# An encoder layer with 32 experts: the experts' tokens gathered in f32 instead of three bf16 parts, and a third place for weights outside the ring

## The chip, the cores and the metric

The kernel runs on one core of a Trainium2 chip. The metric is the device time of one execution in microseconds (us), the median of three timed runs. One further execution was profiled.

## The reference

One encoder layer over 256 tokens of width 1024, all in float32:

```
n = rms_norm(h);  z = n @ w_in                      # 1024 -> 2336 columns
o = concat(bidirectional gated linear attention, grouped-query attention)
h = h + o @ w_out
x = rms_norm(h);  logits = x @ w_router + b_router  # 32 experts
top 4 of 32 experts per token, softmax over the 4
for each expert e, over the tokens that chose it:
    a = x @ w1[e] + b1[e]                           # 1024 -> 2048: glu | lin
    glu = min(a[:, :1024], 7);  lin = clip(a[:, 1024:], -7, 7)
    y = (glu * sigmoid(1.702 * glu) * (lin + 1)) @ w2[e] + b2[e]
h = h + sum over a token's experts of gate * y
out = rms_norm(h)
```

The weights of the experts are 32 x 12.58 MB = 402.7 MB, all of which are read from HBM once.

## The kernel before

**Stages.** The projections and both attentions run first, from 0 to about 120 us. The output projection adds into `h` (2 tiles of 128 tokens, kept in f32 in SBUF), the router picks the experts, and then the 32 experts run one after the other. Each takes up to 64 of its tokens (`CAP`); further rounds would follow if an expert had more, and there are none here.

**Chunks and places.** The weights of an expert come in six chunks of 2 MB (four of `w1`, two of `w2`; chunk c belongs to expert c // 6). `ring` has eight places (`SLOTS`). A place is free again when TensorE has used its chunk and raised `chunk_used`; SyncE waits for that and issues the next load. Its loads are processed in order. Chunks 0 to 7 are loaded before the experts start, each as soon as the part of `ring` that `w_in` or `w_out` held is free. Two more places lie in `work`: `EARLY = 2` chunks, 19 and 20 (`EARLY_AT`), go there, also before the experts start. They are used once. So chunks 8 to 18 wait for the chunk 8 before them, chunks 21 to 28 for the one 10 before them (`SLOTS + EARLY`), and from chunk 29 on (`PEELED`) each waits for the chunk 8 before it again. The first two bodies of four experts (48 chunks) are written out; from chunk 48 a loop loads pairs of 4 MB; the last body is written out again, its last three chunks in halves. In the last body, experts 28 and 29 also add rows to the output (`add_row` L1511, `add_h` L1550), four times each.

**The gather.** TensorE gathers an expert's tokens with a one-hot matrix: weights are 128 tokens x 128 columns of the normed `h`, the moving operand is `onehot` (128 tokens x 64 places), the result 128 x 64 in a PSUM bank, for 8 column groups (`KD`) and 2 token tiles. Column groups take every fourth column, to match how `w1`'s rows lie in the chunks. To keep f32 precision with bf16 matmuls, the normed `h` is held as the sum of three bf16 parts (`PARTS`): `part0` in `work`, the other two in `tok`. So a gather is 8 x 3 x 2 = 48 matmuls (L1543). The parts are made ahead of expert 0: token tile 0 by ACT (L595), DVE (L993) and POOL (L453, L455), tile 1 in halves by ACT (L605, L610) and DVE (L1005, L1011). The first gather is in quarters (`first_gather(half, t)`, L1529): three before expert 0 starts, the fourth after its first chunk. DVE multiplies the result with the norm's gain into `xg` (L1065; L1073 for the first).

**One expert on TensorE.** Bias (L1471), 64 passes of the first layer (L1641), the gather of the next expert, the combine of the last one's result (L1555), the turns of the hidden values (L1667, once DVE's L1095 is done) and of the gates (L1676), 32 passes of the second layer (L1685). Meanwhile DVE clips (L1089, L1090), multiplies (L1092, L1095) and makes the masks (L1082, L1058), and ACT takes the sigmoid (L620) into `sig`. Before the first gather TensorE runs four matmuls whose result isn't used (`keep_busy`, L1477). The router's sum is one matmul per token tile (L1437).

Of the kernel before, what the change touches and what calls it, by code (L numbers as in the profile page):

```python
# [22 lines left out]
BF16 = mybir.dt.bfloat16  # L23
# [45 lines left out]
EARLY = 2  # L69
EARLY_AT = 19  # L70
FINE = (3, 4, 5)
# [12 lines left out]
assert W2_RUN * P == FF and (WRITTEN * PER_BODY - EARLY) % PAIR == 0  # L84
# [34 lines left out]
def encoder_layer(nc, x, w_in, w_out, w_router, w1, b1, w2, b2, gate_w, columns, rows, final_g,  # L119
                  c_keep, c_front, later, split, out):  # L120
    ctx = ExitStack()
    with ctx:
# [19 lines left out]
        wr_sb = sb("wr_sb", [P, KD, EXPERTS])  # L142
        col = sb("col", [P, 2 * KD + 4])
# [6 lines left out]
        class Carve:  # L150
# [70 lines left out]

        early = [work[:, KD * SEQ + i * SLOT:KD * SEQ + (i + 1) * SLOT] for i in range(EARLY)]

# [6 lines left out]
        onehot = back(TILES * CAP // 2).bitcast(BF16).rearrange("p (t c) -> p t c", c=CAP)  # L230
        gated = back(TILES, P)
        gatedT = back(TILES, P)
        xg = back(KD * CAP)
        assert back.at <= KD * SEQ

        back = Carve(work, KD * SEQ + EARLY * SLOT)
# [3 lines left out]
        sig = back(FG)  # L240
        hidT = back(SUB, P)
        part0 = back(TILES * D // 2).bitcast(BF16).rearrange("p (t d) -> p t d", d=D)
        part_sb = back(TILES, P)
        gateT = part_sb.rearrange("p t c -> p (t c)")
        res = back(D // GROUPS)
        reuse = Carve(work, at_glu)
        left = reuse(TILES, D)
# [3 lines left out]
        parts12 = tok.bitcast(BF16).rearrange("p t (i d) -> p t i d", i=PARTS - 1)  # L251
        parts = [[part0[:, t, :]] + [parts12[:, t, i, :] for i in range(PARTS - 1)] for t in range(TILES)]
        hT = [turned[:, :, 0:P], tok[:, 1, :].rearrange("p (k t) -> p k t", t=P)]
# [12 lines left out]
            part0_t0 left_t0 part1_t0 part2_t0 part0_t1 left_t1 part1_t1 part2_t1  # L266
# [19 lines left out]
        def slot_of(c):  # L286

            return (c - EARLY) % SLOTS

        def first_slot_of(c):  # L290

            return c % SLOTS
# [9 lines left out]
        def by_row(chunk, width):  # L302

            return chunk.rearrange("p (r n) -> p r n", n=width)
# [3 lines left out]
        def _(sp):  # L308
# [46 lines left out]
            def first_ring(s):  # L355
                load(slot(s), slot_in[s], s // PER_EXPERT, s % PER_EXPERT)
# [13 lines left out]
            for i in range(EARLY):  # L370
# [48 lines left out]
        def _(pool):  # L419
# [28 lines left out]
            for t in range(TILES):  # L448
                pool.wait_ge(S.var2, t + 1)
                rsqrt(stat[:, 4 + t:5 + t], stat[:, 2 + t:3 + t], 1).then_inc(S.rstd2, 1)  # L450
                if t == 0:
                    pool.wait_ge(S.left_t0, 1)
                    pool.tensor_copy(parts[0][1], left[:, 0, :]).then_inc(S.part1_t0, 1)  # L453
                    pool.wait_ge(S.part1_t0, 1)
                    pool.tensor_tensor(parts[0][2], left[:, 0, :], parts[0][1], ALU.subtract).then_inc(S.part2_t0, 1)  # L455
# [6 lines left out]
        def _(act):  # L462
# [113 lines left out]
            def square(t, nb):  # L576
                act.wait_ge(S.h_done, 2 * t + nb + 1)
                cols = slice(nb * 512, (nb + 1) * 512)
                nc.scalar.activation(left[:, t, cols], h[:, t, cols], ACT.Square,
                                     accum_out=stat[:, 8 + 2 * t + nb:9 + 2 * t + nb]).then_inc(S.hsq, 1)  # L580
# [13 lines left out]
            act.wait_ge(S.rstd2, 1)  # L594
            nc.scalar.activation(parts[0][0], h[:, 0, :], ACT.Copy, scale=stat[:, 4:5]).then_inc(S.part0_t0, 1)  # L595
# [5 lines left out]

            act.wait_ge(S.rstd2, 2)
            for nb in range(2):
                cols = slice(nb * 512, (nb + 1) * 512)
                nc.scalar.activation(parts[1][0][:, cols], h[:, 1, cols], ACT.Copy, scale=stat[:, 5:6]).then_inc(S.part0_t1, 1)  # L605
            act.wait_ge(S.parts_ps, 2)
            for nb in range(2):
                cols = slice(nb * 512, (nb + 1) * 512)
                act.wait_ge(S.left_t1, nb + 1)
                nc.scalar.activation(parts[1][1][:, cols], left[:, 1, cols], ACT.Copy).then_inc(S.part1_t1, 1)  # L610
# [34 lines left out]
            for i in range(GROUPS):  # L645
                act.wait_ge(S.glu_ready, final + (i + 1))
                nc.scalar.activation(halves(sig, i), halves(glu, i), ACT.Sigmoid, scale=ALPHA).then_inc(S.sig_ready, 1)
# [24 lines left out]
        def _(dve):  # L672
# [300 lines left out]
            def choose(t):  # L973
# [18 lines left out]
            dve.wait_ge(S.part0_t0, 1)  # L992
            nc.vector.scalar_tensor_tensor(left[:, 0, :], h[:, 0, :], stat[:, 4:5], parts[0][0], ALU.mult, ALU.subtract)\  # L993
                .then_inc(S.left_t0, 1)
# [7 lines left out]
            def left_over(nb):  # L1002
                cols = slice(nb * 512, (nb + 1) * 512)
                dve.wait_ge(S.part0_t1, nb + 1)
                nc.vector.scalar_tensor_tensor(left[:, 1, cols], h[:, 1, cols], stat[:, 5:6], parts[1][0][:, cols],  # L1005
                                               ALU.mult, ALU.subtract).then_inc(S.left_t1, 1)

            def last_part(nb):
                cols = slice(nb * 512, (nb + 1) * 512)
                dve.wait_ge(S.part1_t1, nb + 1)  # L1010
                nc.vector.tensor_tensor(parts[1][2][:, cols], left[:, 1, cols], parts[1][1][:, cols], ALU.subtract)\  # L1011
                    .then_inc(S.part2_t1, 1)

            left_over(0)

            def first_mask(t):
# [3 lines left out]
                nc.vector.tensor_scalar(onehot[:, t, :], slots[:, 0:CAP], rank_t[:, t, 0:1], None, ALU.is_equal)\  # L1020
# [57 lines left out]
            def expert(n):  # L1078
# [16 lines left out]
                nc.vector.tensor_tensor(lin, lin, sig, ALU.mult).then_inc(S.hid_ready, 1)  # L1095
# [5 lines left out]
            last_part(0)  # L1101
            half_out(0, 3)
            left_over(1)
            last_part(1)
# [24 lines left out]
            for i in range(GROUPS):  # L1129
# [7 lines left out]
                nc.vector.tensor_tensor(lin_i, lin_i, halves(sig, i), ALU.mult).then_inc(S.hid_ready, 1)  # L1137
# [35 lines left out]
        def _(pe):  # L1173
# [340 lines left out]
            def rows_of(t, i, k):  # L1514

                c, r = divmod(k, W1_ROWS)
                return parts[t][i].rearrange("p (c m r) -> p c m r", m=P, r=W1_RUN)[:, c // PAIR, :, c % PAIR * W1_ROWS + r]

            def first_gather(half, t):
# [3 lines left out]
                for i in range(PARTS):  # L1523
                    if t == 1:
                        pe.wait_ge((S.part0_t1, S.part1_t1, S.part2_t1)[i], half + 1)
                    elif half == 0:
                        pe.wait_ge((S.part0_t0, S.part1_t0, S.part2_t0)[i], 1)
                    for k in range(half * KD // 2, (half + 1) * KD // 2):
# [225 lines left out]
```

## Time and profile before

| | before |
|---|---|
| median of three timed runs | 1059.65 us (1057.33 to 1059.96) |
| profiled execution | 1057.77 us |
| its span, first to last instruction | 1056.0 us |
| mean granted TensorE clock | 0.985 of full speed |
| TensorE busy with passes / with weight loads | 988.4 us (94%) / 439.8 us (42%) |
| DVE, ACT, POOL busy | 223.9, 119.0, 16.6 us |
| moved by DMA | 421.50 MB, 399 GB/s over the span |

Busy time is the union of an engine's instructions; it says that an engine had something in flight, not that it was at its peak. In the trace PE stands for TensorE's passes and PEld for its weight loads, which overlap the passes.
### The profile page before, as it was taken

The page shows a single profiled execution, that of the slowest core. Times are in us where ns is not written, and L with a number is a line of the kernel's source. Part 1 is how long each engine was busy: PE and PEld are TensorE (multiplying, and loading weights), DVE is VectorE, ACT ScalarE, POOL GpSimd, SP SyncE. Part 2 cuts the span into 40 slices and gives each one's busy share as a digit, 9 for nine tenths or more (in the row PEclk, how much of TensorE's full clock was granted, in tenths as well). Part 3 has the DMA queues.
Part 4 walks back from the last instruction along what each step waited for, and adds up shares of the span by engine and source line. Part 5 has one row for each costly group of instructions (what it writes and reads, how often), then busy time and mean ns, then how long its engine had stood idle before and what let it go on. Part 6 is the DMA issues. An engine that isn't in the chain of part 4 may idle for free.

```text
span 1056.0 us, 13569 instructions
## 1 busy us (share of the span) xinstructions
PE 988.4 (94%) x5863; PEld 439.8 (42%) x5863; DVE 223.9 (21%) x525; ACT 119.0 (11%) x235; POOL 16.6 (2%) x19
## 2 busy tenths in 40 slices
PE   7999999999999998899898999889999898999996
PEld 5745544444444443334333433334333343433442
DVE  1786341111111111111111111011111111101112
ACT  1055130000000000000000000000000000000002
POOL 0010110000000000000000000000000000000000
PEclk9999999999999999999999999999999999999999
DMA  9917869999999999999999999999999999999994
GB/s 357 270 42 319 367 239 431 426 426 422 428 426 434 433 429 429 433 429 434 429 434 429 434 429 433 431 433 429 433 432 432 431 432 433 425 430 426 427 423 185
DMA packets 25233, 421.50 MB, mean 399 GB/s; under 512 B 4176, under 2 KB 4688, under 8 KB 6800
## 3 DMA queue, kind: packets, MB, share of 16 engines
q1 hardware_dynamic: 25200, 421.01, 94.6%
q8 instruction: 26, 0.43, 0.2%
q14 instruction: 7, 0.06, 0.0%
HBM read 419.95 MB, written 1.05 MB: 399 GB/s over the span
## 4 chain that ended last, share of the span: by engine, by line
PE 65%; DMA 29%; ACT 2%; DVE 2%; issue 1%; POOL 1%; SPq 0%; POOLq 0%; DVEq 0%
PE bank L1641 30%; DMA ring<-in_w_dram 29%; PE bank L1685 14%; PE bank L1555 4%; PE bank L1205 3%; PE bank L1543 3%; PE bank L1667 1%; PE bank L1446 1%; PE bank L1277 1%; ACT work L623 1%; PE bank L1374 1%; PE bank L1471 1%; PE bank L1601 1%; PE bank L1246 1%; DMA col<-in_columns_dram 1%
## 5 line engine op out<-in xcount | busy, mean ns | idle before, releaser
L1641 PE MATMUL bank<-ring,work 128*64 128x512 f32 x2016 | 460.7, 609 | 33.2 <-DMA ring<-in_w_dram 33.0
L1641 PEld LDWEIGHTS bank<-ring,work 128*64 128x64 f32 x2016 | 176.7, 139 | 297.1 <-issue 242.2
L1685 PE MATMUL bank<-ring,work 128*64 128x512 f32 x992 | 219.7, 595 | 14.9 <-ACT work L623 14.9
L1089 DVE TENSOR_SCALAR work<-bank 128x512 f32<-128x512 f32 x31 | 21.4, 692 | 687.6 <-PE bank L1641 687.6
L1685 PEld LDWEIGHTS bank<-ring,work 128*64 128x64 f32 x992 | 68.9, 137 | 145.8 <-issue 127.5
L620 ACT ACTIVATE work<-work 128x512 f32<-128x512 f32 x31 | 19.7, 634 | 501.8 <-DVE work L1089 501.8
L1555 PE MATMUL bank<-work 64*128 64x512 f32 x256 | 63.6, 615 | 0.7 <-ACT work L655 0.7
L1543 PE MATMUL bank<-work,tok 128*128 128x64 bf16 x992 | 51.3, 197 | 0.0
L1543 PE MATMUL bank<-work 128*128 128x64 bf16 x496 | 50.0, 197 | 0.0
L1543 PEld LDWEIGHTS bank<-work,tok 128*128 128x128 bf16 x992 | 48.8, 116 | 0.0
L1543 PEld LDWEIGHTS bank<-work 128*128 128x128 bf16 x496 | 36.5, 116 | 24.8 <-issue 24.8
L631 ACT ACTIVATE work<-bank 128x512 f32<-128x512 f32 x31 | 18.5, 597 | 214.6 <-PE bank L1685 214.6
L1555 PEld LDWEIGHTS bank<-work 64*128 64x128 f32 x256 | 22.0, 186 | 18.7 <-issue 15.9
L623 ACT ACTIVATE work<-bank 128x512 f32<-128x512 f32 x31 | 18.5, 597 | 91.6 <-PE bank L1667 91.6
L1667 PEld LDWEIGHTS bank<-ckeep,work 128*128 128x128 f32 x124 | 17.3, 210 | 24.0 <-DVE work L1095 22.5
L1082 DVE TENSOR_SCALAR work<-ckeep,work 128x128 f32<-128x128 f32 x62 | 18.7, 344 | 34.8 <-PE bank L1676 34.8
L427 POOL TENSOR_TENSOR stat<-stat 128x1 f32<-128x1 f32 (+2 forms) x8 | 9.7, 1211 | 959.3 <-DVE stat L682 943.0
L1667 PE MATMUL bank<-ckeep,work 128*128 128x128 f32 x124 | 23.2, 310 | 1.2 <-DVE work L1095 1.2
L1092 DVE SCALAR_TENSOR_TENSOR work<-work 128x512 f32<-128x512 f32 x31 | 21.5, 693 | 1.1
L1095 DVE TENSOR_TENSOR work<-work 128x512 f32<-128x512 f32 x31 | 21.5, 692 | 1.1
L1065 DVE TENSOR_TENSOR work<-bank,ffn_pairs 128x512 f32<-128x512 f32 x31 | 21.2, 684 | 0.0
L1090 DVE TENSOR_SCALAR work<-bank 128x512 f32<-128x512 f32 x31 | 21.1, 681 | 0.0
(221 smaller groups left out, 505.2 us busy)
## 6 DMA issues: line engine op xcount, KB each, us to landing
ring<-in_w_dram SPq DMA_DIRECT2D x60, 4096.0 KB, 29.8
ring<-in_w_dram SPq DMA_DIRECT2D x67, 2048.0 KB, 16.4
ring<-in_w_in_dram SPq DMA_DIRECT2D x8, 1168.0 KB, 15.9
ring<-in_w_dram SPq DMA_DIRECT2D x6, 1024.0 KB, 29.8
work<-in_w_dram SPq DMA_DIRECT2D x2, 2048.0 KB, 14.7
ring<-in_w_out_dram SPq DMA_DIRECT2D x2, 1024.0 KB, 10.7
ring<-in_w_out_dram SPq DMA_DIRECT2D x1, 2048.0 KB, 16.8
h<-in_x_dram SPq DMA_DIRECT2D x2, 512.0 KB, 4.2
```

What stands on the lines that cost most here:

```text
L623: nc.scalar.activation(hidT, bank[5][:, :].rearrange("p (s q) -> p s q", q=P), ACT.Copy)\
L1065: nc.vector.tensor_tensor(xg.rearrange("p (k c) -> p k c", c=CAP), bank[6][:, :].rearrange("p (k c) -> p k c", c=CAP), ffn_pairs.rearrange ...
L1089: nc.vector.tensor_scalar(glu, bank[2][:, :], LIMIT, None, ALU.min).then_inc(S.glu_ready, 1)
L1090: nc.vector.tensor_scalar(lin, bank[5][:, :], LIMIT, -LIMIT, ALU.min, ALU.max).then_inc(S.dve_step, 1)
L1092: nc.vector.scalar_tensor_tensor(lin, lin, 1.0, glu, ALU.add, ALU.mult).then_inc(S.dve_step, 1)
L1095: nc.vector.tensor_tensor(lin, lin, sig, ALU.mult).then_inc(S.hid_ready, 1)
L1205: return mm(o, l, r, start=a and first, stop=z, skip_group_check=True)
L1543: last = mm(bank[6][:, k * CAP:(k + 1) * CAP], rows_of(t, i, k), onehot[:, t, :], start=i == 0 and t == 0, stop=i == PARTS - 1 and t == TI ...
L1555: last = mm(bank[Y[i]][:, :], gatedT[j * CAP:(j + 1) * CAP, t, :], res[j * CAP:(j + 1) * CAP, :], start=start, stop=stop, skip_group_check ...
L1641: last = mm(bank[(2, 5)[g]][j * CAP:(j + 1) * CAP, :], xg[:, k * CAP:(k + 1) * CAP], of_group(chunk[:, r, :], g, j), start=False, stop=k = ...
L1667: last = nc.tensor.transpose(bank[5][:, r * P:(r + 1) * P], apart[:, :, r], ident)
L1685: last = mm(bank[6][j * CAP:(j + 1) * CAP, :], hidT[:, r, s * CAP:(s + 1) * CAP], chunk[:, r, j * 512:(j + 1) * 512], start=s == 0 and r == 0,
```

## The change

The experts' gather reads f32 tokens from `h` itself. The factor 1/rms of a token, which was in the parts, moves into the one-hot columns: they become f32, with 1/rms (`stat[:, 4 + t]`) where there was 1. A gather is 8 x 2 = 16 f32 matmuls, and the three parts are not made. The room of the parts in `tok` and `work` becomes a third place outside the ring (`EARLY = 3`, chunk 21): half of it in `tok`, half in `work`, loaded by two DMAs of 1 MB (`load_split`). SyncE issues them after TensorE has turned the first attention's result (`glaT_ps`), between the loads of ring places 6 and 7. To make room, the sigmoid (`sig`) goes to PSUM bank 2, and the squares of h to PSUM banks 2 and 5. The ring is turned by one place (`TURN`): chunk 7 goes to place 0, chunk c to place c + 1.

```diff
-EARLY = 2
+EARLY = 3
+TURN = 1
...
-        onehot = back(TILES * CAP // 2).bitcast(BF16).rearrange("p (t c) -> p t c", c=CAP)
+        onehot = back(TILES, CAP)
...
             def slot_of(c):
-            return (c - EARLY) % SLOTS
+            return (c - EARLY + TURN) % SLOTS
...
+            def load_split(i):
+                e, r = divmod(EARLY_AT + i, PER_EXPERT)
+                assert r < W1_CHUNKS
+                n = SLOT // W1_ROWS
+                for j in range(W1_ROWS):
+                    at = r % PAIR * SLOT + j * n
+                    sp.dma_start(early_rows[j], rows_of(e, r)[:, at:at + n]).then_inc(early_in[i], 16)
...
             sp.wait_ge(S.att_used, 1)
             first_ring(6)
+            sp.wait_ge(S.glaT_ps, TILES)
+            load_split(EARLY - 1)
             sp.wait_ge(S.h_ps, 2 * TILES)
             first_ring(7)
...
-                nc.scalar.activation(left[:, t, cols], h[:, t, cols], ACT.Square,
+                nc.scalar.activation(bank[MIX[nb]][:, :], h[:, t, cols], ACT.Square,
...
-            act.wait_ge(S.rstd2, 1)
-            nc.scalar.activation(parts[0][0], h[:, 0, :], ACT.Copy, scale=stat[:, 4:5]).then_inc(S.part0_t0, 1)
...
-                nc.scalar.activation(sig, glu, ACT.Sigmoid, scale=ALPHA).then_inc(S.sig_ready, 1)
+                nc.scalar.activation(bank[2][:, :], glu, ACT.Sigmoid, scale=ALPHA).then_inc(S.sig_ready, 1)
...
-                    last = nc.vector.tensor_scalar(onehot[:, t, :], slots[:, 0:CAP], rank_t[:, t, bass.ds(n, 1)], None,
-                                                   ALU.is_equal)
+                    last = nc.vector.tensor_scalar(onehot[:, t, :], slots[:, 0:CAP], rank_t[:, t, bass.ds(n, 1)],
+                                                   stat[:, 4 + t:5 + t], ALU.is_equal, ALU.mult)
...
             first_mask(0)
             first_mask(1)
-            last_part(0)
             half_out(0, 3)
-            left_over(1)
-            last_part(1)
             tables()
...
                 for k in range(KD):
-                    for i in range(PARTS):
-                        for t in range(TILES):
-                            last = mm(bank[6][:, k * CAP:(k + 1) * CAP], rows_of(t, i, k), onehot[:, t, :],
-                                      start=i == 0 and t == 0, stop=i == PARTS - 1 and t == TILES - 1)
+                    for t in range(TILES):
+                        last = mm(bank[6][:, k * CAP:(k + 1) * CAP], tokens_of(t, k), onehot[:, t, :],
+                                  start=t == 0, stop=t == TILES - 1)
```

## Rows read from the trace of the kernel before

**Rows 1.** The page: TensorE's busy time, and GB/s in 40 slices of 26.4 us.
```profile
PE 988.4 (94%) x5863; PEld 439.8 (42%) x5863; DVE 223.9 (21%) x525; ACT 119.0 (11%) x235; POOL 16.6 (2%) x19
...
GB/s 357 270 42 319 367 239 431 426 426 422 428 426 434 433 429 429 433 429 434 429 434 429 434 429 433 431 433 429 433 432 432 431 432 433 425 430 426 427 423 185
```

**Rows 2.** The chain that ended last, in order: start us, us, what.
```profile
170.06 13.79 PE bank L1641 x64
183.84 1.67 PE bank L1543 x48
...
196.34 13.79 PE bank L1641 x64
...
445.59 8.83 PE bank L1641 x32
...
912.47 7.14 PE bank L1641 x32
...
935.59 1.05 PE bank L1511 x2
...
1007.97 1.67 PE bank L1543 x48
...
1020.47 13.79 PE bank L1641 x64
```

**Rows 3.** Who waited for whom: total us, times, longest.
```profile
PE bank L1641 <- DMA ring<-in_w_dram: 33.0, 18, 2.6
```

**Rows 4.** Stretches: length, busy by engine, granted clock, DMA share, GB/s.
```profile
108.00:150.00 42.00, 40.31 (x220) 20.61 (x220) 18.98 (x58) 12.82 (x24) 7.36 (x6) 1.00 0.68 276
...
134.00:143.00 9.00, 7.75 (x106) 5.45 (x104) 6.54 (x25) 3.73 (x8) 3.73 (x3) 1.00 0.61 234
...
445.60:454.40 8.80, 8.80 (x33) 3.07 (x34) 0.00 (x0) 0.00 (x0) 0.00 (x0) 0.81 0.99 428
```

**Rows 5.** Runs of f32 weight loads, timeline of several windows: start us, us, what.
```profile
93.40 0.52 PEld L1360 LDWEIGHTS bank<-ring 64*128 64x128 f32 x8
...
104.78 3.54 PEld L1367 LDWEIGHTS bank<-work 128*128 128x128 f32 x31 [0.24 <-issue]
...
136.58 0.30 PEld L1437 LDWEIGHTS bank<-ckeep,work 128*128 128x128 f32 x2
...
140.05 0.97 PEld L1477 LDWEIGHTS bank<-h,ckeep 128*128 128x128 f32 x8
...
544.28 0.56 PEld L1667 LDWEIGHTS bank<-ckeep,work 128*128 128x128 f32 x4 [0.76 <-DVE work L1095]
```

**Rows 6.** Timeline around the start of the experts.
```profile
140.53 0.19 DVE L1018 SCALAR_TENSOR_TENSOR work<-bank,work 128x32 f32<-128x32 f32 x1
...
142.12 0.32 PE L1529 MATMUL bank<-work,tok 128*128 128x64 bf16 x4 [0.21 <-DVE tok L1011]
...
142.96 3.70 PE L1641 MATMUL bank<-ring,work 128*64 128x512 f32 x16
...
161.08 0.75 PE L1667 MATMUL bank<-ckeep,work 128*128 128x128 f32 x4 [1.16 <-DVE work L1095]
```

**Rows 7.** Loads by SyncE: issues, and landing of those at 135.44 and 245.07.
```profile
118.84 16.93 SPq L346 DMA_DIRECT2D ring<-in_w_dram  x2
...
DMA to landing us min/median/max: 7.3/7.3/7.3
...
245.07 0.33 SPq L346 DMA_DIRECT2D ring<-in_w_dram  x1
...
DMA to landing us min/median/max: 8.9/8.9/8.9
```

**Rows 8.** The page's costliest groups: three of DVE and ACT.
```profile
L1089 DVE TENSOR_SCALAR work<-bank 128x512 f32<-128x512 f32 x31 | 21.4, 692 | 687.6 <-PE bank L1641 687.6
...
L620 ACT ACTIVATE work<-work 128x512 f32<-128x512 f32 x31 | 19.7, 634 | 501.8 <-DVE work L1089 501.8
...
L1082 DVE TENSOR_SCALAR work<-ckeep,work 128x128 f32<-128x128 f32 x62 | 18.7, 344 | 34.8 <-PE bank L1676 34.8
```

More of the change, by code:

```diff
@@ L218, in encoder_layer @@
         w_out_gla = ring[:, 7 * SLOT:8 * SLOT].rearrange("p (k n) -> p k n", n=D)
-        early = [work[:, KD * SEQ + i * SLOT:KD * SEQ + (i + 1) * SLOT] for i in range(EARLY)]
+        early = [work[:, KD * SEQ + i * SLOT:KD * SEQ + (i + 1) * SLOT] for i in range(EARLY - 1)]
+        at_split = KD * SEQ + (EARLY - 1) * SLOT
+        early_rows = [tok.rearrange("p t d -> p (t d)"), work[:, at_split:at_split + SLOT // W1_ROWS]]
         back = Carve(work)
@@ L239, in encoder_layer @@
         lin = back(FG)
-        sig = back(FG)
-        hidT = back(SUB, P)
-        part0 = back(TILES * D // 2).bitcast(BF16).rearrange("p (t d) -> p t d", d=D)
         part_sb = back(TILES, P)
         gateT = part_sb.rearrange("p t c -> p (t c)")
-        res = back(D // GROUPS)
-        reuse = Carve(work, at_glu)
-        left = reuse(TILES, D)
+        hidT = back(SUB, P)
+        left = Carve(work, at_split)(TILES, D)
         assert back.at <= WORK
         b1_wide = tok.rearrange("p t d -> p (t d)")
-        parts12 = tok.bitcast(BF16).rearrange("p t (i d) -> p t i d", i=PARTS - 1)
-        parts = [[part0[:, t, :]] + [parts12[:, t, i, :] for i in range(PARTS - 1)] for t in range(TILES)]
-        hT = [turned[:, :, 0:P], tok[:, 1, :].rearrange("p (k t) -> p k t", t=P)]
+        hT = [turned[:, :, 0:P], Carve(work, at_glu)(KD, P)]
         ffn_pairs = sb("ffn_pairs", [P, KD])
@@ L300, in halves, with row_of @@
             return tile.rearrange("p (m r) -> p m r", r=W2_ROWS)[:, :, i * n:(i + 1) * n]
-        def by_row(chunk, width):
-            return chunk.rearrange("p (r n) -> p r n", n=width)
+        def row_of(chunk, r, width):
+            return chunk[r] if isinstance(chunk, list) else chunk[:, r * width:(r + 1) * width]
         @block.sync
@@ L369, in _ @@
             sp.wait_ge(S.ogla_ps, 1)
-            for i in range(EARLY):
+            for i in range(EARLY - 1):
                 load_early(i)
@@ L600, in _ @@
             router_parts(1)
[L602 to L610, printed above, removed]
             for t in range(TILES):
@@ L646, in _ @@
                 act.wait_ge(S.glu_ready, final + (i + 1))
-                nc.scalar.activation(halves(sig, i), halves(glu, i), ACT.Sigmoid, scale=ALPHA).then_inc(S.sig_ready, 1)
+                nc.scalar.activation(halves(bank[2][:, :], i), halves(glu, i), ACT.Sigmoid, scale=ALPHA).then_inc(S.sig_ready, 1)
                 act.wait_ge(S.hidT_ps, final + (i + 1))
@@ L1000, in _ @@
             choose(1)
[L1002 to L1014, printed above, removed]
             def first_mask(t):
@@ L1522, in first_gather @@
                 pe.wait_ge((S.onehot_first, S.onehot_ready)[t], 1)
-                for i in range(PARTS):
[L1524 to L1528, printed above, removed]
-                        last = mm(bank[(3, 6)[half]][:, k * CAP:(k + 1) * CAP], rows_of(t, i, k), onehot[:, t, :],
-                                  start=t == 0 and i == 0 and k % 4 == 0, stop=t == TILES - 1 and i == PARTS - 1,
-                                  skip_group_check=True)
+                for k in range(half * KD // 2, (half + 1) * KD // 2):
+                    last = mm(bank[(3, 6)[half]][:, k * CAP:(k + 1) * CAP], tokens_of(t, k), onehot[:, t, :],
+                              start=t == 0 and k % 4 == 0, stop=t == TILES - 1, skip_group_check=True)
                 if t == 1:
@@ L1598, in second_layer @@
                 def second_layer(s, r):
-                    chunk = by_row(slot_for(q, W1_CHUNKS + s), D)
+                    chunk = slot_for(q, W1_CHUNKS + s)
                     for j in range(GROUPS):
                         last = mm(bank[6][j * CAP:(j + 1) * CAP, :], hidT[:, r, s * CAP:(s + 1) * CAP],
-                                  chunk[:, r, j * 512:(j + 1) * 512], start=s == 0 and r == 0,
+                                  row_of(chunk, r, D)[:, j * 512:(j + 1) * 512], start=s == 0 and r == 0,
                                   stop=s == W2_CHUNKS - 1 and r == W2_ROWS - 1, skip_group_check=True)
@@ L1641, in expert @@
                                 last = mm(bank[(2, 5)[g]][j * CAP:(j + 1) * CAP, :], xg[:, k * CAP:(k + 1) * CAP],
-                                          of_group(chunk[:, r, :], g, j), start=False, stop=k == KD - 1,
+                                          of_group(row_of(chunk, r, 2 * FF), g, j), start=False, stop=k == KD - 1,
                                           skip_group_check=True)
@@ L1681, in expert @@
                 for s in range(W2_CHUNKS):
-                    chunk = by_row(loaded(q, W1_CHUNKS + s, it, final_body), D)
+                    chunk = loaded(q, W1_CHUNKS + s, it, final_body)
                     for r in range(W2_ROWS):
@@ L1685, in expert @@
                             last = mm(bank[6][j * CAP:(j + 1) * CAP, :], hidT[:, r, s * CAP:(s + 1) * CAP],
-                                      chunk[:, r, j * 512:(j + 1) * 512], start=s == 0 and r == 0,
+                                      row_of(chunk, r, D)[:, j * 512:(j + 1) * 512], start=s == 0 and r == 0,
                                       stop=s == W2_CHUNKS - 1 and r == W2_ROWS - 1, skip_group_check=True)
```

46 lines of the change are left out of this document (21 added, 25 removed).

## The prediction

> **What bounds the kernel now.** The engine summary and the 40 slices come first [rows 1]: the reader is to see TensorE busy for 94% and the transfers near 430 GB/s in nearly every slice from the seventh on. Two resources are close to full, so a share of busy time decides nothing, and the chain in order of time comes next [rows 2]. In the early experts it holds compute alone. One expert there takes 196.34 - 170.06 = 26.28 us: 13.79 for the first layer, 1.67 for the gather (the piece at 183.84), and the rest. Later, pieces "DMA ring" come in ahead of first-layer pieces like that of 445.59, and TensorE finds a chunk missing once in two experts. The waits list books 33.0 us of it [rows 3]. The rest is the clock: in 445.60 to 454.40, after such a wait, 0.81 was granted [rows 4], and 32 passes took 8.83 us instead of 7.14 [rows 2]. Together they are what is left when compute is taken out: expert 31's first layer starts at 1020.47, 850.4 us after expert 1's. Thirty experts at 26.28 are 788.4, and the extra rows of the last body add eight times 1.05 [rows 2] = 8.4; 850.4 - 796.8 = 53.6 us were lost to waits and slow clock. The transfers set that pace: 912.47 - 445.59 = 466.9 us for 16 experts, 29.18 each. So TensorE has 2.9 us to spare per expert in the middle. It has none in the first experts, before such waits begin, and none after 912.47, where the chain is TensorE to the end. What an added microsecond per expert costs must be read from these three stretches.
>
> **The gather.** Before, 48 bf16 pairs of load and pass take 1.67 us, 35 ns each. After, there are 8 x 2 f32 matmuls. Each f32 matmul of the trace is two load-and-pass pairs (records of the router sum, one matmul: x2), so 32 pairs, with 128 weight columns and 64 streamed ones. Is a pair priced by its load or its pass? [rows 5] The busy time of a run of n loads, less one load's 0.19, over n - 1 gives their spacing. L1477: (0.97 - 0.19)/7 = 0.111 us; L1367: (3.54 - 0.19)/30 = 0.112, both with 128 streamed columns. L1437, with 32, still 0.11 (0.30 - 0.19). L1360, with the very 64 columns, has eight loads in two row halves at a time: (0.52 - 0.19)/3 = 0.11. The stream can shrink and the spacing stays: the load sets it. One thing differs. The new weights are tokens at every fourth element. L1667 (the turns of `lin`) reads its weights with that step: its four loads span 0.56, with 0.20 to 0.22 for one, so 0.115 to 0.12 a gap. I take 0.121, its upper side, since it is the only f32 row with the step. That is 32 x 0.121 = 3.87 us, 2.20 more per gather. Bounds: 0.111 (3.55 us, 1.88 more) and 0.131 (4.19, 2.52 more), twice the surcharge of L1667 on L1477. Below stands the pass alone: at 7.14 us for 32 passes of 512 columns, two column halves at a time [rows 2], a pass is 0.45 us, 0.056 per 64 columns, 1.8 us in all and so no cost; I keep it as a rival.
>
> The Trainium skill ("TensorE: Matmul & The Clock Gate", LDWEIGHTS and weight-path perf modes) says that a load costs its columns over 1.2 GHz, and that a faster load comes on by itself for 128 weights of a type other than FP32. By its rule 128 columns are 107 ns, an estimate of 3.4 us for the gather, and +12 to +14 instead of the +17 below. It speaks against this change just as the rows do.
>
> **Start of the experts.** DVE's two L1005 pieces, L1011 and their partners on ACT and POOL go. In the chain they held the first one-hot until 140.53 and TensorE for 0.21 us at 142.12 [rows 6]. Nothing is won by the first: TensorE's four busy-keeping matmuls (loads from 140.05 at 0.111) last to 141.0 anyway. Three quarter-gathers (24 pairs x 0.121 = 2.9) then end at 143.9 where expert 0 began at 142.96 [rows 6]: +1.0 (bounds +0.7 and +1.2). The halves' scaling on DVE (0.42) ends at about 143.6 and hides. The fourth quarter after chunk 0 is 0.97 against about 0.5: +0.5. Expert 0's own gather is 2.2 longer, but TensorE waited 1.16 there for DVE's L1095 [rows 6], and the turns can't start before the gather and that wait both end: +1.0.
>
> **The third place.** Its 2 MB go as two issues on SyncE between the loads of 118.84 and 135.44 [rows 7]; the window 108 to 150 moves 276 GB/s [rows 4], so it lands near 134 in idle time and delays neither. The stream of the experts then is one chunk (29.18/6 = 4.86 us) shorter. But the stream is short of places, not of time, once: chunk 30 reuses the place of chunk 22, in expert 3's second layer. Its issue at 245.07 lands 8.9 us later, against 7.3 for a load into an idle queue [rows 7]: the queue had all but run dry. After the change chunk 30 still waits for chunk 22, so the lead of the third place is spent there as an idle queue. Worth: 0.0 to 0.3 us.
>
> **The same release, later.** Chunk 22's use moves by 1.0 + 0.5 + 1.0 and three gathers of 2.2, 9.1 us in all. Everything after rides on it: chunk 30 lands at 245.1 + 9.1 + 7.3 = 261.5 instead of 254.0, +7.5, and up to +9.1 for queues that had been idle already. From there transfers need 29.18 per expert and TensorE 26.28 + 2.20 = 28.48, so the stream doesn't run dry again.
>
> **Small parts, all at nothing.** The one-hot with a second scalar and f32 output (L1058) costs at most what L1082's masks with two scalars and twice the columns do, 344 ns [rows 8]; it runs under the second layer. The sigmoid of L620 (634 ns) now writes PSUM and the last product of `lin` reads it; L1089 reads PSUM in 692 ns [rows 8], as that product took from SBUF. Both end before TensorE is through its combine, and the longer gather adds 2.2 us to that cover; without it, a slower sigmoid would count in full. The squares of h into PSUM lie under the output projection.
>
> **The sum** is the later of two lines. TensorE alone: 1.0 + 0.5 + 1.0 + 30 x 2.20 = 68.5, less the 53.6 of waits and slow clock that it swallows, +14.9. Transfers: the last wait, at 912.47, moves by 7.5 to 9.1, and four longer gathers follow it (the last at 1007.97 [rows 2]): 8.8 more, +16.3 to +17.9. I take +17. The profiled execution took 1057.77 us (span 1056.0, 1.8 outside it); the median of the three timed runs is 1059.65, 1.9 above. 1057.8 + 17 = 1074.8; I say 1075.
>
> With 0.111 the two lines give +4.9 and +13.6 to +15.2, with 0.131 +24.9 and about +19: 1071 to 1083. At 2.2 nearly all spare time of the middle is used up; beyond it each 0.1 us more per gather costs 3 us.
>
> **Rivals.**
> *Priced by passes (5%).* The other side: if loads hide under the 56 ns passes, the gather stays at 1.8 us, expert 0 starts 0.5 us earlier, and chunk 30 holds the rest: 1057. For it: the count of matmuls falls by three. Against: L1437 and L1360 [rows 5]. It decides if the spacing is under some 60 ns.
> *The stream is the only bound (10%).* If chunk 30's release doesn't bind, the middle absorbs 2.2 of 2.9 us, the third place takes off 4.9, the start adds 1.0 and the tail 8.8: 1062.7. With cheap passes too it would be 1052, the one way to faster (3% of the ten). Against: 8.9 beside 7.3 [rows 7].
> *A clock fall in each gather (3%).* A thin gather could cost the half-speed stretch of [rows 4], 1.7 us (8.83 - 7.14), in each expert: +50, near 1125. Against: 134 to 143, with short matmuls and waits between them, was granted 1.00 [rows 4].
> *No overlap of load and pass (2%).* A pair would be 0.121 + 0.056 = 0.177, a gather 5.7 us, TensorE's line +70: 1128. Against: L1367 and L1477 fit a load and a pass of 128 columns (a quarter of 0.45) into 0.112 [rows 5]. The Trainium skill ("TensorE: Matmul & The Clock Gate", Part 3, The mechanism) says that loads overlap passes only in other row groups; by that rule this rival would hold, and the trace disagrees.
>
> **Chances.** The forecast and its bounds 80%, the rivals 5, 10, 3 and 2. The range for 8 in 10: 1068 to 1083. 0.3% is 3.2 us, about what runs of this kernel differ by: faster 3%, same 5%, slower 92%.
>
> **What the profile after would show.** Gather pieces near 3.9 us x32 in the chain, at a spacing of 0.12; TensorE's period 28.5 us in the early experts; transfers that stand idle for 8 to 11 us before chunk 30; waits for the ring down from 33.0 to a few us, and granted clock near 1.0 throughout; 13 to 18 us more in all. It is wrong if the spacing is not 0.11 to 0.13, if the queue isn't idle before chunk 30, or if long waits for the ring stay.

## The result, and the profile after

The changed kernel takes 1253.48 us (median of 4 runs, 1250.90 to 1253.99) against 1058.84 for the kernel before (4 runs, 1057.33 to 1059.96): ratio 1.1841, 95% interval 1.1824 to 1.1859. The direction was right, the size was not: +194.6 us where +17 was forecast, far outside 1068 to 1083. The profiled execution took 1250.90 us, with a span of 1249.0.

The page after: TensorE and its loads, granted clock and GB/s in 40 slices of 31.2 us, and the costliest groups of the gather (L1510) and of the first layer (L1609, where L1641 was):

```profile
PE 1218.0 (98%) x5351; PEld 647.4 (52%) x5351; DVE 225.9 (18%) x520; ACT 114.4 (9%) x230; POOL 13.6 (1%) x17
...
PEclk9999888888899988888888899988888888998889
...
GB/s 347 192 264 334 206 318 366 363 174 399 385 363 323 362 367 363 360 370 353 386 403 369 369 361 361 367 355 369 358 364 369 386 403 367 405 362 305 300 279 51
...
L1609 PE MATMUL bank<-ring,work 128*64 128x512 f32 x2000 | 440.5, 596 | 0.0
...
L1510 PEld LDWEIGHTS bank<-work,h 128*128 128x128 f32 x992 | 233.9, 328 | 24.6 <-issue 24.5
```

The waits for the ring are gone (0.0 behind L1609, where [rows 3] had 33.0) and the transfers have fallen from about 430 GB/s [rows 1] to about 365: TensorE alone is the bound. The group to stop at is L1510's loads: 328 ns each, where one f32 load took 190 ns (L1477) to 210 ns (L1667) before.

The chain that ended last, in order (start us, us, what), at the start and for one expert in the middle:

```profile
138.91 5.47 PE bank L1498 x24
144.38 5.64 PE bank L1609 x16
...
502.04 7.66 PE bank L1510 x32
509.70 3.71 PE bank L1522 x8
...
522.46 13.78 PE bank L1609 x64
536.24 7.66 PE bank L1510 x32
```

From gather to gather is 536.24 - 502.04 = 34.20 us, against 26.28 [rows 2]. The gather takes 7.66 us instead of 1.67, +5.99, and the combine behind it (L1522) 3.71. The first layer is unchanged. The three quarter-gathers at the start take 5.47 us, where 2.9 was forecast.

Two stretches of this kernel (length, busy by engine, granted clock, DMA share, GB/s), the first 5 us of a gather and the 6.8 us after them:

```profile
502.10:507.00 4.90, 4.90 (x22) 4.90 (x22) 2.64 (x4) 0.60 (x1) 0.00 (x0) 0.98 1.06 451
...
507.07:513.90 6.83, 6.83 (x24) 4.18 (x24) 0.85 (x2) 0.00 (x0) 0.00 (x0) 0.52 0.95 408
```

Some 5 us into the gather the clock falls to the lower of its two levels, 1.2 GHz, and stays there through the combine. The chain shows the same in every expert: the combine behind a gather takes 3.66 to 3.71 us in all but one (3.19). So two things are new: loads that come half as often as forecast, and a clock fall behind them.

### The profile page after: what moved, and what is told of

It reads as the page before. It is cut to its first block, busy times and chain, and to the rows that moved or that the text cites. A ratio compares the mean times of both kernels' runs of the same rounds, so it can differ in the third digit from the quotient of the medians.

```text
span 1249.0 us, 12532 instructions
## 1 busy us (share of the span) xinstructions
PE 1218.0 (98%) x5351; PEld 647.4 (52%) x5351; DVE 225.9 (18%) x520; ACT 114.4 (9%) x230; POOL 13.6 (1%) x17
## 4 chain that ended last, share of the span: by engine, by line
PE 95%; ACT 2%; DVE 1%; issue 1%; POOL 0%; DMA 0%; SPq 0%; POOLq 0%; DVEq 0%
PE bank L1609 36%; PE bank L1510 19%; PE bank L1653 18%; PE bank L1522 9%; PE bank L1179 3%; PE bank L1635 2%; ACT work L616 2%; PE bank L1445 1%; PE bank L1420 1%; PE bank L1251 1%; PE bank L1348 1%; PE bank L1498 1%; PE bank L1569 1%; PE bank L1220 1%; POOL stat L435 0%
## 5 line engine op out<-in xcount | busy, mean ns | idle before, releaser
L1609 PE MATMUL bank<-ring,work 128*64 128x512 f32 x2000 | 440.5, 596 | 0.0
L1609 PEld LDWEIGHTS bank<-ring,work 128*64 128x64 f32 x2000 | 177.8, 137 | 242.7 <-issue 236.2
L1510 PEld LDWEIGHTS bank<-work,h 128*128 128x128 f32 x992 | 233.9, 328 | 24.6 <-issue 24.5
L1510 PE MATMUL bank<-work,h 128*128 128x64 f32 x992 | 239.4, 415 | 0.0
L1653 PE MATMUL bank<-ring,work 128*64 128x512 f32 x992 | 221.4, 599 | 14.3 <-ACT work L616 14.3
L1522 PE MATMUL bank<-work 64*128 64x512 f32 x256 | 116.9, 1060 | 0.7 <-ACT work L648 0.7
L613 ACT ACTIVATE bank<-work 128x512 f32<-128x512 f32 x31 | 18.7, 602 | 463.2 <-DVE work L1066 463.2
L1522 PEld LDWEIGHTS bank<-work 64*128 64x128 f32 x256 | 36.7, 311 | 37.7 <-issue 32.6
L1059 DVE TENSOR_SCALAR wr_sb<-ckeep,work 128x128 f32<-128x128 f32 x62 | 18.7, 344 | 114.5 <-PE bank L1644 114.4
L1072 DVE TENSOR_TENSOR work<-work,bank 128x512 f32<-128x512 f32 x31 | 21.3, 687 | 1.1
L1445 PE MATMUL bank<-biases,sel 96*64 96x512 bf16 x128 | 20.0, 389 | 0.0
L1179 PE MATMUL bank<-ring,work 128*128 128x32 f32 (+2 forms) x80 | 19.6, 395 | 0.0
```

The costliest lines, as they stand in the source:

```text
L1072: nc.vector.tensor_tensor(lin, lin, bank[2][:, :], ALU.mult).then_inc(S.hid_ready, 1)
L1179: return mm(o, l, r, start=a and first, stop=z, skip_group_check=True)
L1445: mm(bank[(2, 5)[g]][j * CAP:(j + 1) * CAP, :], sel, of_group(b1_parts, g, j), start=True, stop=False, skip_group_check=True)
L1510: last = mm(bank[6][:, k * CAP:(k + 1) * CAP], tokens_of(t, k), onehot[:, t, :], start=t == 0, stop=t == TILES - 1)
L1522: last = mm(bank[Y[i]][:, :], gatedT[j * CAP:(j + 1) * CAP, t, :], res[j * CAP:(j + 1) * CAP, :], start=start, stop=stop, skip_group_check ...
L1609: last = mm(bank[(2, 5)[g]][j * CAP:(j + 1) * CAP, :], xg[:, k * CAP:(k + 1) * CAP], of_group(row_of(chunk, r, 2 * FF), g, j), start=False ...
```

## The experiments

**1. Without the third place.** The changed kernel with two places outside the ring.

```
-EARLY = 3
+EARLY = 2
-TURN = 1
+TURN = 0
...
-            sp.wait_ge(S.glaT_ps, TILES)
-            load_split(EARLY - 1)
```

> The changed kernel with two places outside the ring instead of three (the third is not loaded, the ring not turned); the f32 gather stays. Theory P: TensorE is the only bound after the change (one ring wait is left in its chain), so a place more or less for the transfers moves nothing: 1250 to 1257 us, ratio to the changed kernel 0.998 to 1.002. Rival Q: the third place gives back one chunk's transfer, 4.9 us: 1258 us or more.

Measured: 1251.49 us (4 runs), ratio to the kernel before 1.1829, interval 1.1795 to 1.1864, and 0.998 of the changed kernel: theory P. The place neither gains nor costs anything here. Where TensorE is the only bound, this says nothing of its worth where the transfers are; runs 9 and 10 do.

**2. The same gather, without the step.** One line: the weights are 128 tokens' columns side by side.

```
-                c, r = divmod(k, W1_ROWS)
-                return h[:, t, :].rearrange("p (c m r) -> p c m r", m=P, r=W1_RUN)[:, c // PAIR, :, c % PAIR * W1_ROWS + r]
+                return h[:, t, k * P:(k + 1) * P]
```

> The changed kernel, but each gather matmul takes 128 neighbouring columns of h as weights instead of every fourth one (the output columns are then in the wrong order; nothing else changes). Theory S, the step: loads go back from 0.233 to 0.112 us apart, a gather takes 3.6 us, no clock fall, 1068 to 1076 us. Rival C, the thin f32 gather itself lowers the clock: spacing 0.112 but a slow stretch in each expert, 1110 to 1130 us. Rival F, f32 weights beside a 64-column pass are slow whatever their step: spacing stays 0.233, 1250 us.

Measured: 1076.09 us (one run), clock 0.994: theory S, at the upper end of its times. Its chain, in order:

```profile
139.84 5.01 PE bank L1497 x24
144.85 5.79 PE bank L1608 x16
...
500.66 3.71 PE bank L1509 x32
504.37 1.92 PE bank L1521 x8
```

The step alone carries the loss: without it the gather is 3.71 us (forecast: 3.87), the combine is back at 1.92, and the clock stays up in the experts. Count, type and streamed columns are the same in both. The 5.01 and 5.79 us at its start are another matter (run 5).

**3. The load by step.** The changed kernel with groups of 16 identical matmuls behind its last combine, apart by four wide matmuls each, with 64 streamed columns unless said otherwise.

```
+            for _ in range(16):  # f32 step 4
+                mm(bank[7][:, 0:64], flat32[:, 0:128 * 4].rearrange("p (m r) -> p m r", r=4)[:, :, 0], onehot[:, 0, :], start=True, stop=True)
```

> The changed kernel with test groups of 16 matmuls each on TensorE after its last combine (results unused), four wide matmuls between groups: f32 weights of 128 columns from h at steps of 1, 2, 3, 4, 8 and 16 elements with 64 streamed columns; step 4 with 128 and with 512 streamed columns, from xg instead of h, and with 64 weight columns; transposes at steps 1 and 4; bf16 weights at steps 1, 2, 4, 8 and 16. Theory S: the spacing of f32 loads rises with the step, 0.11 at 1 and 0.23 at 4, the same from h and from xg and with any stream shorter than the load; transposes 0.11 and 0.12. Rival F: 0.23 at every step. Rival H, the place of h in SBUF: 0.23 from h, 0.12 from xg. For bf16 an open question: 0.033 at step 4 is known; if the step counts in bytes, step 8 (16 bytes) is about twice that.

Measured: 1385.69 us (one run), and of the loads by form (x | busy us, mean ns | idle before): f32 with steps of 1, 2, 3, 4 and 8 elements (L1684, L1687, L1690, L1693, L1696), step 4 with 128 streamed columns (L1702), from `xg` in place of `h` (L1708), and with 64 weight columns (L1711):

```profile
L1696 PEld LDWEIGHTS bank<-work,h 128*128 128x128 f32 x32 | 7.8, 334 | 0.4 <-issue 0.2
L1693 PEld LDWEIGHTS bank<-work,h 128*128 128x128 f32 x32 | 7.6, 329 | 0.4 <-issue 0.2
L1708 PEld LDWEIGHTS bank<-work 128*128 128x128 f32 x32 | 7.6, 329 | 0.4 <-issue 0.2
L1702 PEld LDWEIGHTS bank<-ckeep,h 128*128 128x128 f32 x32 | 7.6, 329 | 0.4 <-issue 0.2
...
L1690 PEld LDWEIGHTS bank<-work,h 128*128 128x128 f32 x32 | 5.8, 264 | 0.4 <-issue 0.4
L1687 PEld LDWEIGHTS bank<-work,h 128*128 128x128 f32 x32 | 3.9, 196 | 0.5 <-issue 0.5
L1711 PEld LDWEIGHTS bank<-work,h 128*64 128x64 f32 x32 | 3.9, 216 | 0.8 <-issue 0.8
L1684 PEld LDWEIGHTS bank<-work,h 128*128 128x128 f32 x32 | 3.7, 192 | 0.5 <-issue 0.5
```

Transposes with steps of 1 and 4 elements (L1714, L1717) and bf16 with steps of 4 and 8 (L1726, L1729), from the timeline (start us, us, what). The first load of each of these groups stands apart behind a wide matmul, so these are runs of 15:

```profile
1355.32 1.67 PEld L1714 LDWEIGHTS bank<-ckeep,h 128*128 128x128 f32 x15 [0.29 <-issue]
...
1360.50 1.88 PEld L1717 LDWEIGHTS bank<-ckeep,h 128*128 128x128 f32 x15 [0.23 <-issue]
...
1373.81 0.58 PEld L1726 LDWEIGHTS bank<-ckeep,h 128*128 128x128 bf16 x15 [0.32 <-issue]
...
1377.86 1.01 PEld L1729 LDWEIGHTS bank<-ckeep,h 128*128 128x128 bf16 x15 [0.29 <-issue]
```

Read as in the prediction, (busy - one load) / (count - 1), the spacing is 0.11 us at step 1, 0.12 at 2, 0.18 at 3, and 0.23 to 0.24 at 4 and 8; at 16 it is 0.22. It doubles once each element lies 16 bytes from the last, and grows no further. bf16 does the same at the same distance in bytes: (1.01 - 0.17)/14 = 0.060 at 16 bytes, (0.58 - 0.12)/14 = 0.033 at 8, and 0.029 at 4. With 64 weight columns the stepped load halves, so the price goes by the column. From `xg` it is the same, so the place of `h` plays no part (rival H), and nor do 64 or 128 streamed columns (L1693, L1702). The f32 transpose, one load per operation where a matmul has two, hardly pays the step: (1.88 - 0.21)/14 = 0.12 against (1.67 - 0.14)/14 = 0.11.

The clock differs between two of these groups that are alike in their loads. The stretches of step 4 with 64 streamed columns (L1693) and with 128 (L1702):

```profile
1269.00:1276.60 7.60, 7.60 (x34) 7.48 (x32) 0.00 (x0) 0.00 (x0) 0.00 (x0) 0.85 0.00 0
...
1306.84:1314.50 7.66, 7.66 (x34) 7.54 (x33) 0.00 (x0) 0.00 (x0) 0.00 (x0) 1.00 0.00 0
```

With 64 the clock falls within the group, as it does at steps 8 and 16 and from `xg` (0.88, 0.94 and 0.79 over the group); with 128 it stays, and with 512 as well. So stepped loads alone don't lower it: all four groups that lost it at a step of 4 or more had thin passes behind them.

The Trainium skill ("Advanced Engine Details and Errata", SBUF Cachelines) says that SBUF is read in lines of 16 bytes and that at least two accesses must hit a line for full speed. The trace agrees for matmul weights: two elements to a line (f32 step 2, bf16 step 4) cost next to nothing (0.118 against 0.112 us, 0.033 against 0.029), one to a line costs double. Another page of the Trainium skill ("SBUF — State Buffer", Door 1: The DMA port swizzle) puts the free reach at 4 fp32; if that means a step of 4, the measured 0.23 us against 0.11 disagrees, and the measurement decides.

**4. The gather spread over the first layer.** One gather matmul (two pairs) after each column half of a row.

```
                             for g in range(2):
                                 last = mm(bank[(2, 5)[g]][j * CAP:(j + 1) * CAP, :], ...)
+                            if not first and not final:
+                                if k == 0 and j == 0:
+                                    gather_start(n + 1)
+                                gather_step(k, j)
```

> The changed kernel, but from expert 1 on the 16 gather matmuls are spread over the first layer, one after every two column halves and two groups (four f32 matmuls); expert 0's stays in one piece. Theory L: the slow loads are taken ahead under passes of 0.43 us, so a gather costs only its own passes, about 1.8 us per expert; TensorE stays dense and the clock full: period 26.5 us early on, 1056 to 1064 us. Rival M: a 128-column load waits for the passes of both column halves, nothing hides: period about 32 us or more, 1200 us and above.

Measured: 1743.86 us (one run), clock 0.994. Rival M's "nothing hides" holds, but at a far higher price than its 32 us: an expert takes 50.6 us. Its chain and the granted clock of 100 us:

```profile
597.06 1.86 PE bank L1610 x4
598.92 0.61 PE bank L1510 x2
```

```profile
600.00:700.00 100.00, 98.38 (x290) 39.38 (x288) 8.96 (x20) 4.14 (x8) 0.00 (x0) 1.00 0.62 252
```

Nothing of the gather hides (2 pairs take 0.61), and the first layer itself doubles: 4 passes take 1.86 us, 0.47 each, where the stream has 13.78/64 = 0.215. The stream gains its pace by running the two column halves beside each other; here a gather matmul, which needs all 128 columns, stands between them. Run 8 tests this. A further 2.8 us in each expert are a wait for DVE, which a gather behind the first layer had covered.

**5. Laid out first.** ScalarE copies h into the order that the weights are read in; the gather reads the copy side by side. Two places outside the ring.

```
+            def lay_out(t, half):
+                cols = slice(half * 512, (half + 1) * 512)
+                nc.scalar.activation(tok[:, t, cols].rearrange("p (r m) -> p r m", m=P),
+                                     h[:, t, cols].rearrange("p (m r) -> p r m", r=W1_RUN), ACT.Copy).then_inc(S.laid_out, 1)
...
+                return tok[:, t, k * P:(k + 1) * P]
```

> The gather in f32 from a copy of h that ScalarE lays out in the order of the gather's weights (four copies of 512 columns, 0.6 us each by estimate, in the router's stretch), the columns one after another; 1/rms stays in the one-hot columns; two places outside the ring. Theory S (only the step between the weight's columns costs): gather of 3.6 to 3.9 us in each expert, clock 0.99, 1072 to 1078 us, ratio to the kernel before about 1.015. Rival P (reading f32 tokens from where they lie is not the matter, another cost of the change shows once the column order is right): 1085 or more. Second rival F (the laid-out copy frees enough to win): under 1058.

Measured: 1071.64 us (4 runs, before 1058.76), ratio 1.0127, interval 1.0103 to 1.0152; theory S, 0.4 us below its range (1072 to 1078). Its chain:

```profile
139.18 2.63 PE bank L1505 x24
141.81 3.63 PE bank L1616 x16
...
523.78 3.72 PE bank L1517 x32
527.49 1.92 PE bank L1529 x8
```

The whole of the change's purpose, one f32 gather instead of three bf16 parts, so costs 13 us even with its columns side by side. The other stepless kernel (run 2) is 4.5 us slower, and the start shows why: the same 24 pairs took 5.01 us there and 2.63 here. The stretch 140.00 to 144.80 of run 2, and of this one:

```profile
140.00:144.80 4.80, 4.80 (x25) 4.68 (x24) 1.42 (x7) 0.00 (x0) 0.00 (x0) 0.50 0.01 2
```

```profile
140.00:144.80 4.80, 4.80 (x32) 2.89 (x31) 1.42 (x7) 1.50 (x3) 0.00 (x0) 1.00 0.02 5
```

In run 2 the clock was low there. Why it was, and not here, where the same short matmuls stand ahead of it, isn't shown. The experts began at 144.85 instead of 141.81, and expert 0's first chunk took 5.79 instead of 3.63, 5.2 us in all.

**6. As long, without the step.** Contiguous weights and every gather matmul done twice.

```
                 for k in range(KD):
+                    for again in range(2):
                     for t in range(TILES):
```

> The changed kernel with contiguous weight columns (wrong order of the output's columns) and every f32 gather matmul done twice: 64 load-and-pass pairs in each expert at 0.111 to 0.121 us, 7.1 to 7.7 us, as long as the stepped gather (7.66), but without the step. Theory D (the clock falls because the gather lasts long, whatever its weights are): a fall to half about 5 us into each gather, period 33.5 to 34.1 us, clock 0.91, 1230 to 1255 us. Rival T (the clock falls because stepped loads leave TensorE idle between passes; contiguous pairs keep it filled): no fall, clock 0.99, period 29.9 to 32 us, 1180 to 1195 us or less.

Measured: 1183.08 us (one run), clock 0.994. A gather (chain), and the window over it:

```profile
512.59 7.29 PE bank L1510 x64
519.88 1.92 PE bank L1522 x8
```

```profile
512.59:519.88 7.29, 7.29 (x67) 7.22 (x66) 2.67 (x4) 0.60 (x1) 0.00 (x0) 1.00 1.00 429
```

Theory D fails and T holds: a gather of 7.29 us in 64 quick pairs keeps the full clock, one of 7.66 us in 32 slow pairs loses it. The length of the thin stretch isn't what drops it; the step is, where thin passes stand behind the stepped loads: run 3 has the same loads with 128 streamed columns, and there the clock stays. What the chip goes by, no run here shows.

**7. Two half gathers**, after the second chunk of the first layer and at its end.

```
+                    if not first and not final and c == 1:
+                        gather(n + 1, range(KD // 2))
...
-                    gather(n + 1)
+                    gather(n + 1, range(KD) if first else range(KD // 2, KD))
```

> The changed kernel with its stepped gather in two halves, one after the second chunk of the first layer and one at its end: 16 pairs of 0.233 us, 3.8 us, each. Theory D (a thin stretch of over 5 us drops the clock): no fall, clock 0.99, what the slow clock cost is gone (1.85 us in each of 31 experts, about 57 us): 1190 to 1200 us. Rival A (what counts is the share of thin work over the whole expert, not its length in one piece): the falls stay, clock 0.91, 1245 to 1260 us.

Measured: 1258.18 us (one run), clock 0.947. Its chain over three experts:

```profile
491.46 6.92 PE bank L1611 x32
498.39 3.92 PE bank L1511 x16
502.31 8.62 PE bank L1611 x32
...
525.71 6.92 PE bank L1611 x32
...
536.54 8.57 PE bank L1611 x32
...
548.99 2.92 PE bank L1524 x8
...
561.20 6.92 PE bank L1611 x32
...
571.99 7.07 PE bank L1611 x32
...
582.94 1.92 PE bank L1524 x8
...
593.76 6.43 PE bank L1611 x29
```

Theory D fails: pieces of 3.9 us don't stop the falls. Of the three experts, the first has slow passes once (8.62 for 7.07), the second twice (8.57, and a combine of 2.92), the third never. From first layer to first layer they take 34.25, 35.49 and 32.56 us. So the slow clock costs 1.7 to 2.9 us in an expert, and without it the period is 32.56: what the loads alone leave. The mean of the three is (593.76 - 491.46)/3 = 34.10, against 34.20 in the changed kernel. Rival A named the time (1245 to 1260), though the clock is 0.947, not 0.91.

**8. Two gather matmuls after every row**, behind both column halves.

```
                         for j in range(GROUPS):
                             for g in range(2):
                                 last = mm(bank[(2, 5)[g]][j * CAP:(j + 1) * CAP, :], ...)
+                        if not first and not final:
+                            gather(n + 1, range(k, k + 1))
```

> The changed kernel with two gather matmuls (4 pairs) after every row of the first layer, behind both of its column halves; in the spread run they stood between the two halves, and each pass then took 0.43 us where the stream has one every 0.215. Theory J (the passes of the two halves run beside each other, and a gather matmul between the halves took that away): the row's 8 passes take 1.7 to 1.9 us again, the loads add 0.93 us or less to a row, first layer with gather 21 to 23 us, 1190 to 1210 us in all, clock 0.99. Rival B (any gather matmul every few passes breaks the stream, wherever it stands): a row's 8 passes take 2.6 us or more, 1350 us or more. If loads hide behind wide passes: about 1060 to 1080 us.

Measured: 1257.41 us (one run), clock 0.992. Chain:

```profile
494.56 1.87 PE bank L1611 x8
496.43 1.08 PE bank L1511 x4
```

Theory J holds: with the halves adjacent, a row's 8 passes take 1.87 us again (0.234 each) instead of 3.72. The gather still doesn't hide: 4 pairs take 1.08, more than 4 x 0.234 = 0.94. First layer and gather together take 8 x (1.87 + 1.08) = 23.6 us, where the changed kernel takes 13.78 + 7.66 = 21.44 and loses 1.8 behind it to the clock. So the clock can be kept, but that is paid back in breaks of the stream, and my 1190 to 1210 was wrong because it left them out (2.2 us in each expert).

**9. Everything but the gather's price.** The changed kernel with 48 bf16 matmuls on the upper halves of the f32 tokens.

```
+                at = 2 * (t * D + k * P)
+                return h.rearrange("p t d -> p (t d)").bitcast(BF16)[:, at:at + 2 * P].rearrange("p (m r) -> p m r", r=2)[:, :, 1]
```

> The changed kernel, its third place and all its small parts, with a gather as short as the kernel before has: 48 bf16 matmuls that read the upper halves of the f32 tokens 4 bytes apart (0.03 to 0.035 us each, 1.4 to 1.7 us; it leaves out the lower halves of the tokens and the order of the output's columns). Theory G (all of the loss is the gather; the rest of the change is worth nothing, the third place too because chunk 30 waits again for the place of chunk 22): period 26.0 to 26.3 us, the stream is the bound again with about 30 us of waits, 1055 to 1061 us, ratio 0.997 to 1.002. Rival H (other parts cost too, such as ScalarE's sigmoid and square into a bank or the later release of chunks): 1064 us or more. Rival P3 (the third place gives its 4.9 us): 1052 to 1055.5 us.

Measured: 1055.96 us (10 runs, before 1057.55 with 13), ratio 0.9979, interval 0.9966 to 0.9992: theory G.

**10. The same, the three places holding chunks 37 to 39.**

```
-EARLY_AT = 19
+EARLY_AT = 37
```

> The kernel of the short gather with the places outside the ring holding chunks 37 to 39 in place of 19 to 21 (one constant). Theory L (a place loaded ahead saves one transfer, but only if it holds a chunk from the stretch where TensorE has caught up with the stream; at 19 the saving is used up while chunks still lie ready): one transfer of 4.9 us less in the chain, 1050 to 1056 us, ratio 0.993 to 0.997. Rival N (where the places stand in the order makes no difference): as the short gather with 19, within 1 us of it.

Measured: 1051.86 us (4 runs), ratio 0.9945, interval 0.9927 to 0.9964: theory L. Run 9's page and its waits for the ring, with slices of 26.4 us:

```profile
GB/s 357 260 78 317 424 267 411 428 429 354 429 426 437 426 429 437 425 430 436 430 431 433 435 426 431 435 429 431 435 433 428 433 435 428 427 430 425 427 424 186
...
PE bank L1612 <- DMA ring<-in_w_dram: 36.6, 18, 3.2
```

Run 10's, the same two:

```profile
GB/s 358 267 65 319 427 259 408 428 427 427 428 427 436 428 429 433 429 432 430 433 434 429 433 435 428 434 435 428 433 435 429 431 430 434 426 429 427 428 423 166
...
PE bank L1612 <- DMA ring<-in_w_dram: 33.7, 18, 2.6
```

The tenth slice shows where they part: 354 GB/s where the third place holds chunk 21, 427 where it holds chunk 39. The gap, 0.073 MB per us x 26.4 us = 1.9 MB, is the third place's own transfer of 2 MB, won at the start and given back as an idle queue at chunk 30. Moved later, it is kept: 1055.96 - 1051.86 = 4.1 us, of the 4.9 that a chunk takes. With a short gather nothing else in the change shows a cost; the experts begin 2.0 us earlier than in the kernel before (140.93 against 142.96), as the parts aren't made, and a cost of up to that size could hide behind it.

## Why the prediction was wrong

**The gather** is the step that failed. It priced a pair by its load, which is right (7.66 us for 32 pairs, the pass far below), and saw that the weights have a step of 4. It then took the step's surcharge from L1667, "the only f32 row with the step". But L1667 is a transpose, and run 3 shows that an f32 transpose hardly pays a step that a matmul's weights pay in full: 0.12 against 0.23. So the term 32 x 0.121 = 3.87 was 7.66, and the upper bound 0.131, made by doubling that same row's surcharge, was no bound at all. Rows of two kinds of operation were joined as if they were one, and no row of the kernel before reads matmul weights in f32 with a step. A sign that the step does lengthen a load lay in that trace: L1667's take 210 ns each, those of the transposes that read side by side 147:

```profile
L1676 PEld LDWEIGHTS bank<-ckeep,work 128*128 128x128 f32 x6 | 0.8, 147 | 0.0
```

In run 3 the transposes show the same, 208 and 141 ns, at nearly the same spacing. Runs 2 and 5 show the sum was nearly sound for the load it assumed: 1076 and 1072 us. That run 2 came within 1 us of 1075 is partly luck, as it holds 5.2 us of slow clock at the start that the sum had not in it.

**The clock** is the second failure. The rival "a clock fall in each gather" had 3% and a price of 1.7 us in each expert. It came true in every expert, with about that price (combine 3.71 against 1.92), on top of the loads and not in their place. The evidence against it was a stretch with contiguous weights [rows 4], and run 6 shows that inside an expert those keep the clock. So both failures come from the step, the second by way of the thin passes behind it.

**The sum.** From run 5 to the changed kernel the span grows by 1249.0 - 1068.8 = 180.2 us. The longer gather gives 31 x (7.66 - 3.72) = 122, the slow combine 30 x (3.71 - 1.92) = 54 (expert 0 has none), expert 0's turns and second layer, which meet the low clock in its place, 0.87 + 8.78 against 0.53 + 7.09, so 2, the quarter-gathers 5.47 + 2.01 against 2.63 + 1.04, so 4, and expert 0's first chunk 5.64 against 3.63, so 2. That is 184, less the 2.9 us of waits for the ring that run 5 still has: 181. From the kernel before to run 5 it is 12.8: 30 x (3.72 - 1.67) = 61.5 of compute, less most of the 53.6 us that waits and slow clock cost before. The two lines of the prediction work; at "beyond it each 0.1 us more per gather costs 3 us" it even named the slope.

**The third place, and the same release later**, were right. Runs 9 and 10 show the mechanism: the lead is lost as an idle queue before chunk 30. In run 2 the tenth slice (of 26.9 us), with the later release as well, fell to 250 GB/s from some 430: 11 us of an idle queue, where 8 to 11 were forecast.

**Start of the experts.** The three quarter-gathers took 2.63 us without the step at full clock (2.9 forecast) and 5.47 in the changed kernel. That the clock can be low here (run 2 had it too, without the step) was not foreseen, and its cause stays open. **Small parts at nothing** is confirmed by run 9 as a whole, to within the 2.0 us of its earlier start: ratio 0.9979 with all of them in.

**Of the other rivals**, "priced by passes" and "no overlap" are refuted by the 3.71 us of run 2. "The stream is the only bound" (1062.7) is refuted by run 2, which has the third place: 1076.09, of which the slow start explains 5.2, and its queue stood idle before chunk 30.

## What to carry to other kernels

Before a weight operand is read with a step, count bytes: f32 weights four elements apart cost twice the load of adjacent ones, while bf16 parts four apart cost next to nothing more. An exchange of bf16 for f32 that takes 48 matmuls down to 16 can still make them more than four times as long (1.67 to 7.66 us), through type and step together; and a bound from a transpose is no bound for a matmul. A place that holds data early pays only if it holds what is needed after the stream has become the bound.

## What the runs showed of the hardware that was not expected

- Spacing of f32 weight loads of 128 columns in matmuls: 0.11 us at step 1, 0.12 at 2, 0.18 at 3, 0.23 at 4, 0.24 at 8; bf16 at 16 bytes 0.060 against 0.033 at 8. f32 transposes at step 4: 0.12 against 0.11.
- Contiguous f32 loads follow TensorE's clock: 24 in 2.63 us at a granted 1.00, 24 in 5.01 at 0.50. Stepped ones don't: 24 in 5.47 us at the low clock, 32 in 7.66 with most of them at the high one, 0.23 to 0.24 us each; what limits them isn't shown.
- Inside an expert, thin matmuls keep the full clock over 7.29 us if their loads are contiguous, and lose it after some 5 us if they are stepped. Behind the same stepped loads, 128 streamed columns keep it for 7.66 us (run 3). Why half gathers of 3.9 us lose it in some experts only stays open.
- Stepped f32 loads do hide behind wide passes of their own size: in run 3, 32 pairs at step 4 with 512 streamed columns take 13.7 us, 0.43 each, the pace of the contiguous ones between the groups.
- A matmul of 128 weight columns between two column halves of 64 takes their overlap away: 1.86 us for 4 passes against 1.87 for 8 when it stands behind both.
